# First layer of a two-network kernel: small loads issued by SyncE, tokens turned between modulation chunks, two q quarters as native fp32 products, context scaled by ScalarE

## The reference, cut to what matters

```python
sh1_l, sc1_l, g1_l, sh2_l, sc2_l, g2_l = jnp.split(jax.nn.silu(c) @ ada_w[i] + ada_b[i], 6, axis=-1)
hl = modulate(rms_norm(xl, norm_mix[i]), sh1_l, sc1_l)        # modulate: h * (1 + scale) + shift
sh1_c, sc1_c, ... = jnp.split((jax.nn.silu(c_ctx) @ ada_w[i] + ada_b[i])[None], 6, axis=-1)
hc = modulate(rms_norm(xc, norm_mix[i]), sh1_c, sc1_c)
...
proj = h @ w_in                                               # 1024 x 2576
qkv, z, gates, pool_in = jnp.split(proj, [QKV_W, QKV_W + V_W, QKV_W + V_W + 4 * DN_HEADS], axis=-1)
qkv = jax.nn.silu(dw_conv(qkv, conv_w)).astype(jnp.float32)
```

## Time and profile before

| | |
|---|---|
| median of 3 runs | 1440.92 us (1440.23 to 1444.82) |
| profiled execution | 1444.88 us, its span 1443.2 us |
| TensorE matmul busy | 1225.7 us (85%) |
| TensorE weight load busy | 896.7 us (62%) |
| VectorE busy | 616.7 us (43%) |
| ScalarE busy | 432.4 us (30%) |
| GpSimd busy | 78.2 us (5%) |
| DMA | 338.65 MB, mean 235 GB/s; 409 GB/s through the expert layers |
| chain that ended last | TensorE 63%, DMA 17%, VectorE 10%, SyncE's queue 4%, ScalarE 3%, issue 2%, ScalarE's queue 1% |

### The profile page before, as it was taken

One profiled execution on the slowest core, in us unless ns is written; L12 is line 12 of the kernel. 1 busy time (PEld: TensorE's weight loads), 2 busy tenths in 40 slices (PEclk: granted clock), 3 DMA queues, 4 the chain that ended last, 5 costly groups with the idle time before them and its releaser, 6 DMA issues.

```text
span 1443.2 us, 19524 instructions
## 1 busy us (share of the span) xinstructions
PE 1225.7 (85%) x8265; PEld 896.7 (62%) x8265; DVE 616.7 (43%) x1120; ACT 432.4 (30%) x777; POOL 78.2 (5%) x118
## 2 busy tenths in 40 slices
PE   5899889999976766789998666668999999999887
PEld 3677558786832212359984211225899868899756
DVE  3645784555520000146743000002895366545574
ACT  2436333322300000034231000002454654443562
POOL 3000123530000000000000000000000000000000
PEclk9999899999997667699999767869999979999898
DMA  9844854335789999975467999998145303444000
GB/s 327 312 141 162 292 187 164 117 109 195 283 322 409 409 409 409 409 260 176 176 239 311 409 409 409 409 409 317 62 173 167 126 1 118 174 172 172 9 1 30
DMA packets 125099, 338.65 MB, mean 235 GB/s; under 512 B 8657, under 2 KB 11590, under 8 KB 125014
## 3 DMA queue, kind: packets, MB, share of 16 engines
q1 hardware_dynamic: 117536, 334.51, 61.2%
q10 hardware_dynamic: 7478, 2.91, 0.8%
HBM read 336.35 MB, written 1.05 MB: 234 GB/s over the span
## 4 chain that ended last, share of the span: by engine, by line
PE 63%; DMA 17%; DVE 10%; SPq 4%; ACT 3%; issue 2%; ACTq 1%; DVEq 0%
PE bank L679 9%; PE bank L681 9%; PE bank L680 9%; DMA weight_ring<-in_w_up_dram 7%; PE bank L968 4%; DMA expert_slots<-in_w_down_dram 3%; DMA arena<-in_w_up_dram 3%; DMA weight_ring<-in_w_down_dram 3%; DVE arena L1869 3%; PE bank L993 2%; SPq L1248 2%; PE bank L586 2%; PE bank L1132 2%; PE bank L891 2%; PE bank L947 2%
## 5 line engine op out<-in xcount | busy, mean ns | idle before, releaser
L679 PE MATMUL bank<-input_high,weights_high 128*128 128x256 f32 (+1 forms) x992 | 291.7, 294 | 8.2 <-DVE input_low L1869 7.5
L681 PE MATMUL bank<-input_high,weights_low 128*128 128x256 f32 (+1 forms) x992 | 285.1, 287 | 0.0
L680 PE MATMUL bank<-input_low,weights_high 128*128 128x256 f32 (+1 forms) x992 | 284.9, 287 | 0.0
L1869 DVE TENSOR_TENSOR weights_low<-weight_ring,weights_high 128x1024 fp32r<-128x1024 f32 x144 | 176.1, 1224 | 185.2 <-ACT weights_high L1425 184.8
L679 PEld LDWEIGHTS bank<-input_high,weights_high 128*128 128x128 f32 x992 | 189.6, 191 | 13.4 <-issue 10.6
L1425 ACT ACTIVATE weights_high<-weight_ring 128x1024 fp32r<-128x1024 f32 x144 | 151.7, 1055 | 146.4 <-PE bank L681 146.1
L681 PEld LDWEIGHTS bank<-input_high,weights_low 128*128 128x128 f32 x992 | 189.7, 191 | 0.0
L680 PEld LDWEIGHTS bank<-input_low,weights_high 128*128 128x128 f32 x992 | 189.3, 191 | 0.7
L1869 DVE TENSOR_TENSOR arena<-arena,bank 128x512 f32<-128x512 f32 (+1 forms) x38 | 24.8, 653 | 269.0 <-PE bank L968 238.6
L968 PE MATMUL bank<-weight_ring,arena 128*32 128x512 f32 x512 | 83.7, 796 | 45.9 <-DMA weight_ring<-in_w_up_dram 33.2
L968 PEld LDWEIGHTS bank<-weight_ring,arena 128*32 128x32 f32 x512 | 18.0, 128 | 107.1 <-issue 48.7
(11 more groups left out here) (410 smaller groups left out, 1769.4 us busy)
## 6 DMA issues: line engine op xcount, KB each, us to landing
weight_ring<-in_ada_w_dram SPq DMA_DIRECT2D x24, 2048.0 KB, 8.6
weight_ring<-in_w_gate_dram SPq DMA_DIRECT2D x16, 2048.0 KB, 16.2
weight_ring<-in_w_down_dram SPq DMA_DIRECT2D x16, 2048.0 KB, 21.2
weight_ring<-in_w_up_dram SPq DMA_DIRECT2D x16, 2048.0 KB, 24.4
weight_ring<-in_even_w_in_dram SPq DMA_DIRECT2D x9, 2048.0 KB, 9.3
arena<-in_w_up_dram SPq DMA_DIRECT2D x8, 2048.0 KB, 20.2
expert_slots<-in_w_up_dram SPq DMA_DIRECT2D x8, 2048.0 KB, 23.9
arena<-in_w_gate_dram SPq DMA_DIRECT2D x8, 2048.0 KB, 23.6
```

The costliest lines, as they stand in the source:

```text
L679: pe.matmul(b[:, 0:width], hi[:, k, :], XHI[:, k, t0:t0 + width], start=k == 0, stop=False)
L680: pe.matmul(b[:, 0:width], hi[:, k, :], XLO[:, k, t0:t0 + width], start=False, stop=False)
L681: mm = pe.matmul(b[:, 0:width], lo[:, k, :], XHI[:, k, t0:t0 + width], start=False, stop=k == KD - 1)
L1869: return dve.tensor_tensor(out_, a, b, op)
```

## The change

It has five parts.

1. The 25 small loads are issued by SyncE, behind the k weights and ahead of modulation chunk 4, no longer by ScalarE.
2. TensorE turns the tokens right behind chunk 0. Then each of chunks 1 to 3 is preceded by the turn of the one before and four warm matmuls; the last turn follows. `ada_copy` and `ada_bias` are moved to match. The transposes of meta tokens and vectors go behind the q product (`late_vectors`), and 6 warm matmuls stand ahead of it instead of 10.
3. The first two q quarters are native fp32 matmuls of the weights as they are with `hT`, eight to a quarter; only quarters 2 and 3 are split. The slot of the q weights is now released when the q product is through. The splits in ScalarE's and VectorE's loops move by two places, and the tables' exponentials, the copy of the meta tokens and a memset move behind.
4. VectorE scales all eight latent tiles first, then makes their low parts. The context is scaled by ScalarE, twice: once into the high part, once in place; VectorE makes the low parts only.
5. The order of the stream is: modulation chunks 0 to 3, q, k, chunk 4, v, chunks 5 and 6, z, pool, chunks 7 to 9.

```diff
...
         first_vec_in, vec_in, small_in, meta_in = sem("first_vectors_in"), sem("vectors_in"), sem("small_in"), sem("meta_in")
         x_in, ctx_in, tokens_ready = sem("x_in"), sem("context_in"), sem("scaled_tokens_ready")
         first_split, context_high, masks_ready = sem("first_input_split"), sem("context_high_part"), sem("masks_ready")
+        context_scaled = sem("context_scaled")
         router_in, poolw_in, dtw_in = sem("router_in"), sem("pool_w_in"), sem("dt_w_in")
         consts_ready = sem("constants_ready")
         c_exp, c_ready = sem("c_exp"), sem("silu_c_ready")
...
         QKV = 3 * 512
         ada_at = [0, 1, 2, 3]
         W_EV = []
-        for src, adas in (((ev, 0), 1), ((ev, 512), 1), ((ev, 1024), 1), ((ev, QKV), 0), ((ev, QKV + 512 + 16), 3)):
-            W_EV.append(len(stream))
-            stream += [cols(*src)]
-            for _ in range(adas):
-                ada_at.append(len(stream))
-                stream += [ada_src[len(ada_at) - 1]]
+        for src in ((ev, 0), (ev, 512), None, (ev, 1024), None, None, (ev, QKV), (ev, QKV + 512 + 16), None, None, None):
+            (ada_at if src is None else W_EV).append(len(stream))
+            stream += [ada_src[len(ada_at) - 1] if src is None else cols(*src)]
         for i in range(len(ada_at), 24):
             ada_at.append(len(stream))
             stream += [ada_src[i]]
...
                     s_close(mm, ("norm", i))
             ada_mm()
-            ada_mm()
-            pe.wait_ge(scalar_drained, ada["copied"] - 1)
-            ada_turn()
             for tt in range(2 * TT):
                 pe.wait_ge(tokens_ready, tt + 1)
                 for kh in range(2):
                     b = s_open() if tt % 2 else v_open()
                     mm = transposes(b, [(b[:, k * P:k * P + P], XN[:, tt, (4 * kh + k) * P:(4 * kh + k + 1) * P]) for k in range(4)])
                     (s_close if tt % 2 else v_close)(mm, ("tokens", tt))
-            for i in range(2):
+            for i in range(3):
+                pe.wait_ge(scalar_drained, ada["copied"])
+                ada_turn()
+                warm(4)
                 ada_mm()
-                pe.wait_ge(scalar_drained, ada["copied"] - 1)
-                ada_turn()
             pe.wait_ge(scalar_drained, ada["copied"])
             ada_turn()
-
-            pe.wait_ge(meta_in, 16)
-            b = s_open()
-            for k in range(KD):
-                mm = pe.transpose(b[:, k * META:(k + 1) * META], MIN[0:META, k * P:(k + 1) * P], ident[0:META, 0:META])
-            s_close(mm, "meta")
-
-            pe.wait_ge(vec_in, 16 * (n_vec - len(first_vecs)))
-            vec_transposes((1, 2), "more_vecs")
-
+            def late_vectors():
+
+                pe.wait_ge(meta_in, 16)
+                b = s_open()
+                for k in range(KD):
+                    mm = pe.transpose(b[:, k * META:(k + 1) * META], MIN[0:META, k * P:(k + 1) * P], ident[0:META, 0:META])
+                s_close(mm, "meta")
+                pe.wait_ge(vec_in, 16 * (n_vec - len(first_vecs)))
+                vec_transposes((1, 2), "more_vecs")
             def ada_step():
...
                 cn = W_EV[i]
-                for m in range(4):
+                if i == 0:
+                    arrive(cn)
+                    for m in range(2):
+                        b = opener()
+                        for k in range(KD):
+                            if m == 0:
+                                pe.wait_ge(h_scaled, k + 1)
+                            mm = pe.matmul(b[:, 0:T], chunk(cn)[:, k, m * P:m * P + P], hT[:, k, 0:T], start=k == 0, stop=k == KD - 1)
+                        closer(mm, (names, mt + m))
+                for m in range(0 if i else 2, 4):
                     j = len(quarters)
                     pe.wait_ge(weights_split, j + 1)
                     b = opener()
                     hi, lo = WHI[:, j % 2], WLO[:, j % 2]
                     for k in range(KD):
-                        if j in (0, 4):
-                            pe.wait_ge(first_split, KD * (j // 4) + k + 1)
+                        if (i, m) in ((0, 2), (1, 0)):
+                            pe.wait_ge(first_split, KD * i + k + 1)
                         pe.matmul(b[:, 0:width], hi[:, k, :], XHI1[:, k, 0:width], start=k == 0, stop=False)
                         pe.matmul(b[:, 0:width], hi[:, k, :], XLO1[:, k, 0:width], start=False, stop=False)
                         mm = pe.matmul(b[:, 0:width], lo[:, k, :], XHI1[:, k, 0:width], start=False, stop=k == KD - 1)
...
                     quarters.append((cn, m, scalar_filled if closer is s_close else vector_filled, done))
                     if between is not None and m < 3:
                         between()
-                released[cn] = (weights_split, len(quarters))
+                released[cn] = (weights_split, len(quarters)) if i else (scalar_filled, done)
             def product(cn, mt, width, opener, closer, names, new_input=False, after=None, t0=0):
...
                         after(mt + m)
                 released[cn] = (weights_split, len(quarters))
-            warm(10)
+            warm(6)
             first_product(0, 0, T, s_open, s_close, "qkv")
+            late_vectors()
             ada_step()
             first_product(1, 4, 2 * T, s_open, s_close, "qkv")
             ada_step()
...
                 if cn == 2:
                     sp.wait_ge(x_in, 16)
                     sp.wait_ge(ctx_in, 16)
+                if cn == W_EV[1] + 1:
+                    for name in vec_src:
+                        if name not in first_vecs:
+                            g, r, k = vec_at[name]
+                            sp.dma_start(VEC[r:r + k, g, :], vec_src[name]).then_inc(vec_in, 16)
+                    sp.dma_start(MIN[0:META, :], meta_2).then_inc(meta_in, 16)
+                    for dst, src in small_src:
+                        sp.dma_start(dst, src, allow_slow_non_contiguous=True).then_inc(small_in, 16)
                 free_slot(cn)
                 if stream[cn][0] == "lru":
                     half = slot(cn).rearrange("p (g b k n) -> p g b k n", g=2, b=4, k=2)
...
                 if j == mark[("split", n["segment"])]:
                     return
                 cn, m, _, _ = quarters[j]
-                if m == 0:
+                if m == 0 or j == 0:
                     act.wait_ge(landed[slot_of(cn)], landed_at(cn))
                 if j >= 2:
                     act.wait_ge(quarters[j - 2][2], quarters[j - 2][3])
...
                 n["high"] += 1
-            def load_vecs(names, signal):
-                for name in names:
-                    g, r, k = vec_at[name]
-                    act.dma_start(VEC[r:r + k, g, :], vec_src[name]).then_inc(signal, 16)
-
-            load_vecs(first_vecs, first_vec_in)
+            for name in first_vecs:
+                g, r, k = vec_at[name]
+                act.dma_start(VEC[r:r + k, g, :], vec_src[name]).then_inc(first_vec_in, 16)
             for s, (src, signal) in enumerate(((x, x_in), (ctx, ctx_in))):
                 act.dma_start(XIN[:, 2 * s:2 * s + 2, :], src[0].rearrange("(t p) n -> p t n", p=P)).then_inc(signal, 16)
...
             then(act.activation(trs, tsum, ACT.Ln, bias=EPSC, scale=1.0 / D))
             act.activation(trs, trs, ACT.Exp, scale=-0.5).then_inc(rstd_ready, 1)
-            act.dma_start(MIN[0:META, :], meta_2).then_inc(meta_in, 16)
-            load_vecs([name for name in vec_src if name not in first_vecs], vec_in)
-            for dst, src in small_src:
-                act.dma_start(dst, src, allow_slow_non_contiguous=True).then_inc(small_in, 16)
             ada = [0]
             def ada_copy():
...
                 ada[0] += 1
             ada_copy()
-            ada_copy()
             for tt in (1, 3):
                 for kh in range(2):
                     b = take()
                     drained(act.activation(hT[:, 4 * kh:4 * kh + 4, tt * P:tt * P + P], bank(b, 4, P), ACT.Copy))
-            ada_copy()
-            ada_copy()
-
-            def first_high(c0, signal):
-
-                for k in range(KD):
-                    scaled_tiles[0] += 1
-                    act.wait_ge(h_scaled, scaled_tiles[0])
-                    act.activation(XHI1[:, k, c0:c0 + T], hT[:, k, c0:c0 + T], ACT.Copy).then_inc(signal, 1)
-
-            first_high(0, h_ready)
+            for _ in range(3):
+                ada_copy()
+
+            for k in range(KD):
+                scaled_tiles[0] += 1
+                act.wait_ge(h_scaled, scaled_tiles[0])
+                act.activation(XHI1[:, k, 0:T], hT[:, k, 0:T], ACT.Copy).then_inc(h_ready, 1)
             high()
             high()
-            first_high(T, context_high)
-            act.wait_ge(small_in, 16 * n_small)
-            act.activation(alog, alog, ACT.Exp)
-            act.activation(salog, salog, ACT.Exp)
-            b = take()
```

(70 more changed lines are left out.)

## The result

The change made the kernel slower: 1457.03 us in the median (1450.58 to 1459.89, 4 runs) against 1440.93, a ratio of 1.0112 with a 95% interval of 1.0079 to 1.0146. Forecast were 1433.5 us, between 1429.5 and 1438. The profiled execution took 1450.58 us (span 1448.8), the shortest of the four; where it differs from the median is told at the end.

What follows compares the result with a forecast made beforehand. TensorE was taken as bound by its late start, behind ScalarE's DMA issuing. Earlier start 5.3, stall and slow clock 3.6, less 0.9, gave 8.0 us; less 0.5, 7.5 off 1440.9, say 1433.5, range 1429.5 to 1438.

Steps and rivals of the forecast that it cites:

- Small loads leave ScalarE: At the start: chunk 0's copy can run at 19.3 us, and the tokens take 4.7 us, to 24.0.
- tokens between chunks: Three rounds of 5.1 us after the tokens: last turn at 39.3, scaling starting at 40.8, only 0.2 us sooner.
- two native quarters: Start of the q product: TensorE starts at 42.75, against 48.07; two native quarters cost 6.9 us instead of 5.6.
- the split quarters: Rest of the q product: quarters 2 and 3 run from 49.65 to 55.3 us with no stall.
- late vectors: Meta and vector transposes behind the q product: 0.9 us, now uncovered, before chunk 4 and the k product at 58.0.
- Context on ScalarE: During the q product: 16 activations at 0.33 us each, 5.3 in all; first k quarter's low part at 54.8, costing nothing.
- What waits in SyncE's queue: Before chunk 4: 25 loads cost at most 7.0 us, chunk 4 lands by 54.4, wanted at 56.2; stall taken as 0.
- (b): Rival before chunk 4: small loads cost some 11 us in line, stall 2.2, gain only 3.6, 1437 us; chance 0.13.
- (d): Rival in SyncE's queue: chunks 4 and later hang behind the 25 issues; at 22 us, 1446 us; chance 0.07.
- The removed splits in the loop: Convolution loop: removed splits, moved memset and exponentials have several us of cover per tile.
- (c): Rival: SyncE or the rounds hold TensorE, or the gain goes into a later wait; 1440 us; chance 0.08.
- Is it kept to the end?: From the k product to the end: nothing absorbs the 8.0 us gain; less 0.5 for small waits, 7.5.

Runs made afterwards that it cites:

- e6: The e4 kernel with the context scaled by VectorE again, ScalarE making only the high parts: 1427.61 us, ratio 0.9867.
- e8: The e4 kernel measured again, on one chip with e9 and in more rounds: 1429.31 us, ratio 0.991.
- e9: The e6 kernel (context scaled by VectorE) measured again beside e8: 1431.94 us, ratio 0.992.
- e3: The changed kernel with the two ssd_d loads issued behind the pool weights and waited for only where used: 1443.52 us, ratio 1.0017 to the kernel before.
- e1: The changed kernel with VectorE making two more low parts ahead, its convolution loop splitting from tile 1, not 3: 1441.04 us, ratio 1.0012 to the kernel before.
- e2: The kernel before the change, with VectorE leaving out the low parts of its first two loop passes: 1457.34 us, ratio 1.0119.
- e4: The changed kernel with the edits of e1 and e3 together: 1432.76 us, ratio 0.9942 to the kernel before.

## Why the prediction was wrong

Point by point, by its own steps.

*Small loads leave ScalarE; tokens between chunks; two native quarters; the split quarters; late vectors.* Right, each within 0.4 us from the last turn on: tokens from 20.0 to 24.2, turn at 39.33, native at 42.57, split at 49.29, late vectors done at 56.3. The two native quarters took 6.72 (6.9 forecast). One reason in it does not hold: the work on chunk 0 was to raise the clock for the tokens, but the profile of the kernel before grants 1.00 on chunk 0 too (15.6 to 19.3 us), although its matmuls took 3.64. That the tokens ran fast was forecast rightly; why chunk 0 is slow stays open.

*Context on ScalarE.* A mis-sized term that cost nothing. The timeline of ScalarE in the changed kernel:

```profile
45.72 2.06 ACT L1524 ACTIVATE first_input_high<-arena,modulation,small 128x256 fp32r<-128x256 f32 x4
47.82 2.08 ACT L1529 ACTIVATE arena<-arena,modulation,small 128x256 f32<-128x256 f32 x4
```

0.52 for one, against the 0.33 that I took from a plain copy, 8.3 us in all and not 5.3. The Trainium skill (ScalarE: Activation LUTs, What ACT_TABLE_LOAD costs) gives 93 ns for each scale or bias that is read by pointer; two of them make up the 0.19 measured. The low part of the first k quarter was ready at 56.2, still ahead of TensorE; e6, e8 and e9 agree.

*What waits in SyncE's queue.* This step failed. It priced the 25 loads by what they had taken from the large chunks, at most 7.0 us, and took 0 for the stall. In line they cost 14.5: k weights landed at 44.6 (issue 28.5 and 16.1 to landing), chunk 4 at 64.4, and 5.3 of the 19.8 between are its own. By e3, 2.2 of the 14.5 belong to 23 loads and some 12 to the two of ssd_d. The trace of the kernel before held the answer in three places: the last piece of ScalarE's issuing, 2.91 us for the last load, an ssd_d load; the 0.56 of the DMA engines from 38 to 43 us, which the prediction read and spread over all 25 loads; and its list of DMA issues of the first 230 us (count, KB each, median us to landing; the other tables take 11):

```profile
small<-in_ssd_d_dram ACTq DMA_DIRECT2D x2, 2.0 KB, 17.5
```

On ScalarE's queue nothing stood behind them that anyone waited for, and the weights in SyncE's queue went on, though at less than half their rate (last section); on SyncE's queue the weights stood behind them. So the 7.0 us did not only change place, as the prediction had it: they became 14.5. My bound came from the time that the large chunks had lost, and what ran out was the queue's time. With e3 the term is what I had taken, no stall.

*Rivals (b) and (d)* had the right place. (d) named 17 us in line as the point from which the change is slower; with 14.5 and a late k chunk it gave +2.0 at the k product, the half clock included. I gave (d) 0.07 and (b) 0.13, with the argument that ScalarE issued them in 13.4 us; SyncE did in 16.9 (28.95 to 45.8), but issuing is not moving.

*The removed splits in the loop.* This step failed worst, in half a sentence: "several us of cover per tile". I compared ScalarE's lists and found them in step (two quarters left for the pool stretch in both). I did not count VectorE's. Before: 4 low parts ahead of the loop, 12 in it, 2 behind, 18 of 20, so 2 are left. Changed: 3, 9 and 2, 14 of 18, so 4 are left. Two quarters fewer need splitting, but four calls were taken out: three in the loop and one ahead of it. That four low parts left over make a ring of waits was nowhere in the prediction. The cost is 15 us at a place 70 us behind the code that I was timing; e1 takes it away, and e2 makes it in the kernel before. No rival had this mechanism; (c) said "a later wait" without a place, and priced it at the gain, not beyond it.

*Is it kept to the end?* Right in kind: the 17 us by which the pool stretch ended later (183.97 against 167.00) are still 16 to 17 at the loads of 350 and 615 us. The profiled span ends only 5.6 us later than that of the kernel before, since this execution had its later stretches at a higher granted clock: the first stretch of the second network's products had 0.96 where the one before had 0.90 (1124.8 to 1218.7 and 1112 to 1210 us), and took 4.1 us less. The medians do not share that; two spans of single executions must be compared at their landmarks.

## What to carry to other kernels

When work is taken out of one end of a pipeline that several engines feed by hand-written lists, count what each engine is ahead by at the far end, for every engine and not for one: a list that falls two steps behind can turn overlap into a ring of waits, here 15 us, far from the edit. When a load moves to another queue, price what stands behind it there by the load's own time from issue to landing, not by the bytes or the engines' busy share. A change with a good idea and two oversights measures as a bad one: with both repaired it is 0.6 to 0.9% faster (e4, e8). The timelines explain 9 us of it (0.6%); the median of e8 lies 14.4 below the kernel before in its series, while its k product (57.31) and its decay rows (158.25) come 8.75 us sooner, and the rest is open.

## What was new about the hardware

Two loads of 512 single floats each held the DMA queue of the engine that issued them for about 10 us, with the 16 DMA engines at 0.05 of their time and 3 GB/s, while 2 MB stood behind them in the same queue. The low share is no sign of a free DMA: packets of 4 bytes take little of it and still keep the queue.

In the kernel before the same two loads were in ScalarE's queue and the weights in SyncE's. There the weights did not stop, but they were slowed. The trace has the 4-byte packets of ScalarE's queue from 33 us to the landing of the last load at 44.7. While they went at full number, from 36 to 44 us, the DMA engines moved 174 GB/s; as soon as they were through, 403 (columns as in the earlier trace rows):

```profile
36.00:44.00 8.00, 7.25 (x52) 4.70 (x51) 4.31 (x18) 3.09 (x7) 0.00 (x0) 1.00 0.62 174
44.00:46.00 2.00, 1.75 (x8) 1.12 (x6) 2.00 (x8) 1.44 (x4) 0.00 (x0) 1.00 1.05 403
```

In those 8 us the two queues (q1 is SyncE's, q10 ScalarE's; packets, MB, share of 16 engines) had nearly the same number of packets, 2 KB in one and 4 bytes in the other, as if they took turns:

```profile
q1 hardware_dynamic: 696, 1.39, 58.3%
q10 hardware_dynamic: 648, 0.00, 3.9%
```

So a load of single elements costs the weights beside it more than half their rate, and those behind it everything, as long as it lasts.

An activation of 128 x 256 that takes scale and bias from SBUF took 0.52 us, where a plain copy of the same size takes 0.33.
